# Transposing finished activation blocks with VectorE and device memory instead of TensorE, with four raw weight slots

## The reference, cut to what matters

```python
for l in range(2):
    h = rmsnorm(x, norm_mix[l])
    qa, ka, va, qi, ki, wi, qb, kb, vb = split(h @ w_in[l])
    o_a = dsa_branch(...)          # 8 heads x 128; keys chosen by an indexer score (qi, ki, wi), top 64 of 256
    o_b = swa_branch(...)          # 16 heads x 64, 2 kv heads, window of 128 keys, sinks
    g_a, g_b = split(sigmoid(h @ w_gate[l]))
    merged = g_a * (o_a @ w_branch_a[l]) + g_b * (o_b @ w_branch_b[l])
    x = x + merged @ w_out[l]
    h = rmsnorm(x, norm_mlp[l])
    x = x + square(relu(h @ w_up[l])) @ w_down[l]      # hidden width 8192
return rmsnorm(x, final_norm)
```

## Time and profile before

| | |
|---|---|
| median of 3 runs | 2830.13 us (2829.62 to 2831.28) |
| profiled execution: span, first to last instruction | 2829.1 us |
| TensorE busy / weight loads busy | 98% / 79% of the span |
| VectorE / ScalarE / GpSimd busy | 53% / 44% / 0% |
| mean granted TensorE clock | 0.994 |
| DMA | 506.41 MB, 54.1% of 16 engines' time |

### The profile page before, as it was taken

How to read it: one execution, slowest core, us unless ns; L and a number is a source line. 1 busy time by engine, 2 the same in 40 slices (tenths; PEclk the granted TensorE clock), 3 DMA queues, 4 the chain that set the end, 5 groups by cost and what they waited for, 6 DMA issues and landing times.

```text
span 2829.1 us, 37435 instructions
## 1 busy us (share of the span) xinstructions
PE 2784.3 (98%) x12610; PEld 2246.4 (79%) x12610; DVE 1503.9 (53%) x2106; ACT 1248.0 (44%) x1622; POOL 6.5 (0%) x16
## 2 busy tenths in 40 slices
PE   5999999999999999999999999999999999999998
PEld 4878778888888888888887887788888888888886
DVE  4575554555555555545555655545555455455554
ACT  3445454444444434434444455544444344343443
POOL 0000000000000000000000000000000000000000
PEclk8999999999999999999999999999999999999999
DMA  7644545555555555555554544455555555555553
GB/s 244 218 166 157 164 156 179 184 180 183 181 186 186 178 187 184 183 187 181 168 192 164 178 149 164 161 187 180 185 180 179 188 183 185 182 181 186 185 181 117
DMA packets 144951, 506.41 MB, mean 179 GB/s; under 512 B 15644, under 2 KB 21820, under 8 KB 144700
## 3 DMA queue, kind: packets, MB, share of 16 engines
q1 hardware_dynamic: 144828, 504.80, 54.1%
HBM read 497.92 MB, written 6.82 MB: 178 GB/s over the span
## 4 chain that ended last, share of the span: by engine, by line
issue 96%; DMA 2%; PE 1%; DVE 0%; ACT 0%; SPq 0%; POOL 0%; DVEq 0%; POOLq 0%; ACTq 0%
DMA raw<-in_w_main 1%; PE acc L340 0%; PE acc L341 0%; PE acc L342 0%; DMA bias_b<-bias_rows 0%; DMA raw<-in_w_misc 0%; DVE xs L1280 0%; ACT h_hl L766 0%; ACT w_hi L653 0%; DVE w_lo L918 0%; SPq L232 0%; SPq L258 0%; POOL bias_b L299 0%; POOL bias_b L298 0%; POOL root L291 0%
## 5 line engine op out<-in xcount | busy, mean ns | idle before, releaser
L918 DVE TENSOR_TENSOR w_lo<-raw,w_hi 128x1024 fp32r<-128x1024 f32 (+1 forms) x944 | 1146.5, 1218 | 1156.9 <-ACT w_hi L653 1153.5
L653 ACT ACTIVATE w_hi<-raw 128x1024 fp32r<-128x1024 f32 (+1 forms) x944 | 993.3, 1054 | 1317.5 <-PE acc L342 1279.0
L340 PE MATMUL acc<-w_hi,h_hl 128*128 128x512 f32 x2176 | 874.5, 402 | 20.2 <-DVE w_lo L918 20.2
L342 PE MATMUL acc<-w_hi,h_hl 128*128 128x512 f32 x2176 | 860.0, 395 | 0.0
L341 PE MATMUL acc<-w_lo,h_hl 128*128 128x512 f32 x2176 | 859.6, 395 | 0.0
L340 PE MATMUL acc<-w_hi,o_hl 128*128 128x512 f32 x1408 | 560.0, 398 | 0.0
L342 PE MATMUL acc<-w_hi,o_hl 128*128 128x512 f32 x1408 | 556.3, 395 | 0.0
L341 PE MATMUL acc<-w_lo,o_hl 128*128 128x512 f32 x1408 | 555.9, 395 | 0.0
L340 PEld LDWEIGHTS acc<-w_hi,h_hl 128*128 128x128 f32 x2176 | 409.7, 188 | 117.6 <-DVE w_lo L918 21.1
L342 PEld LDWEIGHTS acc<-w_hi,h_hl 128*128 128x128 f32 x2176 | 409.2, 188 | 97.8
L341 PEld LDWEIGHTS acc<-w_lo,h_hl 128*128 128x128 f32 x2176 | 409.9, 188 | 92.1
(11 more groups left out here) (141 smaller groups left out, 1029.7 us busy)
## 6 DMA issues: line engine op xcount, KB each, us to landing
raw<-in_w_main SPq DMA_DIRECT2D x928, 512.0 KB, 3.3
raw<-in_w_misc SPq DMA_DIRECT2D x16, 336.0 KB, 5.7
bias_rows<-stage SPq DMA_DIRECT2D x1, 4608.0 KB
xs<-in_x SPq DMA_DIRECT2D x4, 512.0 KB, 6.2
out<-xs SPq DMA_DIRECT2D x4, 512.0 KB, 2.9
bias_b<-bias_rows SPq DMA_DIRECT2D x1, 1536.0 KB, 11.5
bias_a<-bias_rows SPq DMA_DIRECT2D x1, 1024.0 KB, 7.2
qk<-in_final_gain SPq DMA_DIRECT2D x1, 1024.0 KB, 5.2
```

The source lines that it names most:

```text
L340: nc.tensor.matmul(o, a_hi, hi[:, kk], start=(k == 0), stop=False)
L342: last = nc.tensor.matmul(o, a_lo, hi[:, kk], start=False, stop=fin)
L653: nc.scalar.activation(w_hi[s][:, 0:2 * width], raw[r][:, 0:2 * width], ACT.Copy).then_inc(hi_ready, 1)
L918: nc.vector.tensor_tensor(w_lo[s][:, 0:2 * width], raw[r][:, 0:2 * width], w_hi[s][:, 0:2 * width].bitcast(F32), ALU.subtract).then_inc(lo ...
```

## The change

TensorE no longer transposes anything after the start (the fourth quarter of x in each layer's narrow chunks stays on it). Instead:

- In `take`, right behind the work that finishes the block, DVE transposes it in 32x32 blocks from [128 tokens, 512] into the tile `spread`, one instruction for each of the two token tiles (`spread_block`; `spread_keys` for the small keys). The output is written with elements 32 bytes apart.
- SP stores `spread` (512 KB, rows of 4 KB) to a device-memory tensor `scratch`, ahead of its load of chunk 7, and after its load of chunk 7 waits for the store and issues four fetches, each to 32 partitions in runs of 1 KB (`pass_on`). They land in the q/k tiles directly, or in `moved`.
- After their split of chunk 6 (hook `taken`), ACT makes the hi part from `moved` and DVE the lo part, for the whole block at once (`hi_moved`, `lo_moved`; for x, with its gains, in four pieces, `hi_moved_x`, `lo_moved_x`).
- The moved layout is [token, token tile, piece]: one channel block's 128 tokens lie 8 floats (32 bytes) apart. All stationary operands but the attention outputs are read with that stride, in the start's blocks too; so are queries and keys in the attention products, the small keys 16 bytes apart. `b_logits` makes its second key block with two matmuls instead of one.
- `RAW` is 4 instead of 8, to make room for `spread` and `moved`. SP's loads are written out by unit (`load_unit`), not in a loop of 8. The holds are at chunks 0 and 6.
- The 36 moves of a layer are 1 of keys, 8 of q/k columns, 27 of others (4 merged, 4 + 3 of x, 16 of the MLP).

```diff
-RAW = 8
+RAW = 4
+PIECES = NB // P
+QUARTERS = P // 32
...
-        h_hl = sb("h_hl", [P, 2, KT, SEQ], F32R)
+        h_hl = sb("h_hl", [P, 2, NBLK, P, TT, PIECES], F32R)
-        qk = sb("qk", [P, 2, A_HEADS, SEQ])
+        qk = sb("qk", [P, 2, 2, P, TT, PIECES])
+        kiT_kbT = sb("kiT_kbT", [P, P, TT, 2])
+        spread = sb("spread", [P, QUARTERS, 32, TT, PIECES])
+        moved = sb("moved", [P, P * TT * PIECES])
+        scratch = nc.dram_tensor("scratch", (P, NB * TT), F32, kind="Internal")
...
+            def load_unit(l, at, chunks, passing=None):
+                for c in range(chunks):
+                    if c == 7 and passing:
+                        passing[0]()
+                    sp.wait_ge(lo_ready, at + (l * CHUNKS + c + 1))
+                    sp.dma_start(raw[c % RAW][:], w_main[l, at + (c - N_MISC)]).then_inc(raw_in[c % RAW], 16)
+                if passing:
+                    passing[1]()
+            def pass_on(l, e, dst, pieces, g=0):
+                size = pieces * TT * 32
+                def store():
+                    sp.wait_ge(spread_ready, g * NBLK + (l * MOVES + e + 1))
+                    sp.dma_start(bass.AP(scratch, 0, [[NB * TT, P], [1, QUARTERS * size]]),
+                                 spread[:].rearrange("p j s t k -> p (j s t k)")[:, 0:QUARTERS * size]).then_inc(spread_stored, 16)
+                def fetch():
+                    sp.wait_ge(spread_stored, g * (NBLK * 16) + (l * (MOVES * 16) + (e + 1) * 16))
+                    for jj in range(QUARTERS):
+                        sp.dma_start(dst[32 * jj:32 * jj + 32],
+                                     bass.AP(scratch, jj * size, [[NB * TT, 32], [32 * NB * TT, QUARTERS], [1, size]]))\
+                            .then_inc(landed, 16)
+                return store, fetch
...
             def h_lhs(part, k, t):
-                return h_hl[:, part, k, t * P:(t + 1) * P]
+                return h_hl[:, part, k // PIECES, :, t, k % PIECES]
+            def moved_lhs(flat, k, t):
+                return flat.rearrange("p (s t k) -> p s t k", t=TT, k=PIECES)[:, :, t, k % PIECES]
+            def u_lhs(part, k, t):
+                return moved_lhs(o_moved[:, part, k // PIECES], k, t)
...
                 if j == 0:
-                    pe.wait_ge(turn_took, l * TURNS + (T_FIRST + T_QB + 4))
+                    pe.wait_ge(landed, l * (MOVES * LANDED) + (E_QB + 3) * LANDED)
...
-                    last = nc.tensor.matmul(att[g][:, 3 * P - WINDOW_KEYS:3 * P], q[:, P:SEQ], k[:, SEQ - WINDOW_KEYS:],
+                    nc.tensor.matmul(att[g][:, at:at + 64], q[:, :, 1], k[:, 64:P, 0], start=False, stop=False,
+                    last = nc.tensor.matmul(att[g][:, at + 64:3 * P], q[:, :, 1], k[:, :, 1], start=False, stop=True,
...
-                def turn_u(g, n, half):
-                    pe.wait_ge(squared, l * (GROUPS * NBLK) + g * NBLK + (n + 1))
-                    pe.wait_ge(turn_took, l * TURNS + g * 8 + (T_FIRST + T_U + 2 * n + half))
-                    for j in range(2):
-                        for t in range(TT):
-                            last = nc.tensor.transpose(turn[:, (j * TT + t) * P:(j * TT + t + 1) * P],
-                                                       stage_src(stage, half)(j, t), ident[:])
-                    last.then_inc(turned, 1)
...
-                    unit(..., o_lhs, ..., hold=[(0, turn_took, u0 + 6), (6, turn_took, u0 + 7), (7, turn_took, u0 + 8)] ...)
+                    unit(..., u_lhs, ..., hold=[(0, moved_took, g * NBLK + took_of(E_U + 2)), (6, moved_took, g * NBLK + took_of(E_U + 3))] ...)
...
                     split(cl, c, width, phase)
                     if turns and c in (5, 7):
                         turns((c - 5) // 2)
+                    if taken and c == 6:
+                        taken()
...
+            def hi_moved(l, e, dst, scale=1.0, g=0):
+                moved_ready(l, e, g)
+                nc.scalar.activation(dst, moved[:], ACT.Copy, scale=scale).then_inc(moved_hi, 1)
...
+            def spread_block(l, e, src, g=0):
+                spread_free(l, e, g)
+                if e >= E_M:
+                    dve.wait_ge(moved_took, g * NBLK + (l * TAKES + (e - E_M + NBLK)))
+                for t in range(TT):
+                    last = nc.vector.transpose(spread[:, :, :, t, :].rearrange("p j s k -> p k j s"),
+                                               src[:, t, :].rearrange("p (k j s) -> p k j s", k=PIECES, j=QUARTERS))
+                last.then_inc(spread_ready, 1)
+            def lo_moved(l, e, hi, lo, scale=1.0, g=0):
+                dve.wait_ge(moved_hi, g * NBLK + (l * TAKES + (e - E_M + 1)))
+                nc.vector.scalar_tensor_tensor(out=lo, in0=moved[:], scalar=scale,
+                                               in1=hi.bitcast(F32), op0=ALU.mult, op1=ALU.subtract).then_inc(moved_took, 1)
```

More of the change, by code:

```diff
@@ L238, in load_misc @@
                     sp.wait_ge(lo_ready, l * CHUNKS + (c + 1))
[L239 to L246, removed]
+                    sp.dma_start(raw[c % RAW][:, 0:2 * MISC], w_misc[l, c]).then_inc(raw_in[c % RAW], 16)
@@ L653, in split, with unit @@
                 nc.scalar.activation(w_hi[s][:, 0:2 * width], raw[r][:, 0:2 * width], ACT.Copy).then_inc(hi_ready, 1)
-            def unit(cl, chunks, take=None, turns=None, jobs=None, width=NB, phase=0, first=0):
+            def unit(cl, chunks, take=None, turns=None, taken=None, jobs=None, width=NB, phase=0, first=0):
                 for c in range(first, chunks):
@@ L763, in _ @@
                     act.wait_ge(turned, 2 * n + half + 1)
-                    for j in range(2):
-                        k = 4 * n + 2 * half + j
-                        last = nc.scalar.activation(h_hl[:, 0, k, :], first_turn[2 * n + half][:, j * SEQ:(j + 1) * SEQ],
-                                                    ACT.Copy, scale=gain[:, 0, k:k + 1])
-                    last.then_inc(turn_hi, 1)
+                    first_hi(first_turn[2 * n + half], n, half, lambda k: gain[:, 0, k:k + 1])
                 if n < 2:
@@ L848, in x_squares @@
                         square_block(n - 1, l * (2 * NBLK) + (NBLK + n - 1))
-                    unit(l * CHUNKS + (C_OUT + 8 * n), 8, take=x_squares if n else None, turns=x_out_turned)
+                    unit(l * CHUNKS + (C_OUT + 8 * n), 8, take=x_squares if n else None, taken=out_moved)
                 def take_up(g, n):
@@ L944, in hx @@
-            def hx(n, half):
-                return lambda part: h_hl[:, part, 4 * n + 2 * half:4 * n + 2 * half + 2, :]
+                    k = 2 * half + j
+                    hi, lo = (h_hl[:, part, n, :, :, k].rearrange("p s t -> p t s") for part in range(2))
+                    src = b[:, j * SEQ:(j + 1) * SEQ].rearrange("p (t s) -> p t s", t=TT)
+                    last = nc.vector.scalar_tensor_tensor(out=lo, in0=src, scalar=gain_of(PIECES * n + k),
+                                                          in1=hi.bitcast(F32), op0=ALU.mult, op1=ALU.subtract)
```

429 lines of the change are left out of this document (223 added, 206 removed).

## The result

The changed kernel takes 2984.02 us (median of 4 runs, 2982.77 to 2985.78), the kernel before 2830.11 us beside it (4 runs): a ratio of 1.054, 95% interval [1.053, 1.056]. It is slower by 154 us; I had forecast 2786 us and had put the upper end of the range at 2960. The profiled execution's span is 2984.1 us, 155.0 above the one of before.

The account below looks back on a forecast made before the run. TensorE's instruction stream was taken to pace everything; 2829.1 - 61.5 (transposes) + 0 (loads) + 5 (attention) + 3.5 (split) + 7 (start) + 2 (jitter) = 2785.1 us span, forecast 2786 us, range 2766 to 2960.

Parts of the forecast that it names:

- Removed from TensorE: TensorE's stream: 142 groups of four transposes go, each 0.433 us, saving 61.5 us in full.
- The weight loads with 32-byte stride: 10560 strided loads on TensorE stay hidden under matmuls of 0.233 us, up to 2.1 times the present pace: cost 0.
- my upper bound: Strided weight load: 1.82 ns an element, path 0.233 us, record 0.31 us, so 0.08 us exposed each, 845 us more.
- The rival that I gave 0.20: Strided load path exceeds 0.233 us under all 10560 matmuls; priced at 0.04 us each, +422, 3208 us; chance 0.20.
- Attention: Attention products: strided keys and queries as moving operands cost +5 us, at most +40 if reading doubles.
- The split: Mixer B's second key block, split in two, adds 32 matmuls with a load path of 0.11 us each: +3.5 us.
- VectorE: covered: 144 block transposes at 0.9 us (bound 1.4) add some 90 us busy time on an engine 53% busy, no delay.
- The round trip: Store and fetch through device memory land at T+12.3 after TensorE ends a unit at T; no stalls, 2.2 us spare.
- jitter: Allowance of +2 us for the round trip, whose margin was 2.2 us at the holds and 1 us for x blocks.
- comes too late: Rival: fetched blocks land at T+18 instead of T+12.3, stalling TensorE 122 us in all, 2906 us; chance 0.11.
- Four slots: Four raw slots: covered in the steady state; at the start the bias store goes out at about 25, costing +7 us.
- the sign that I gave: Sign of a right forecast at the start: one TensorE wait of about 27 us near the start.

Follow-up runs that it names:

- e7: The kernel before with the bias store issued by ScalarE on its own queue: 2810.6 us, ratio 0.993.
- e9: The changed kernel with blocks moved in runs of 32 tokens, all key, value, hidden and query operands dense, bias store on ScalarE's queue: 2765.1 us, ratio 0.977.
- e1: The changed kernel with the main products' stationary operands read from 128 neighbouring floats, writes and moves unchanged: 2841.4 us, ratio 1.003.
- e10: The changed kernel with the main products' stationary operands read 8 bytes apart, writes and moves unchanged: 2832.2 us, ratio 1.001.
- e3: The changed kernel with the main products' stationary operands read 16 bytes apart, writes and moves unchanged: 2919.1 us, ratio 1.032.
- e8: The changed kernel with queries and keys of the attention products read in neighbouring elements, main products left strided: 2935.6 us, ratio 1.037.
- e6: The changed kernel with blocks moved in runs of 32 tokens, main operands dense, queries strided, bias store on ScalarE's queue: 2793.5 us, ratio 0.987.
- e4: The kernel before with four raw slots instead of eight, bias tiles still behind 24 main chunks: 2838.2 us, ratio 1.003.
- e5: The changed kernel with blocks moved in runs of 32 tokens and main stationary operands written densely, queries still strided: 2814.3 us, ratio 0.994.

## Why the prediction was wrong

**What bounds the kernel, and what is paid ten thousand times: right.** "Anything that lengthens a matmul's distance" was the sentence that decided.

**Removed from TensorE, -61.5: right.** 20 matmuls on `turn` are left, as said. I had measured one group of four; all 142 in the trace of before, each less two matmul distances, sum to 61.8 us. Between e7 and e9, 45.5 us apart, the start distances of the matmuls on `turn` fall by 50.4 us and those of the main products beside them by 10.0; the second mixer's key products (+6.9), the waits for `w_lo` (+6.6) and the narrow chunks (+1.5) take some of it back.

**The weight loads with 32-byte stride, taken as 0: this step failed.** The claim was "up to 2.1 times the present pace it costs nothing", and that was sound; the load's path became 0.245 / 0.11 = 2.2 times as long. What was wrong is the argument for the pace. I took the moving operand's 0.46 ns a column as the pace "at which reading is possible" and concluded that a load has room to stride. But the moving operand of that row has neighbouring elements; it shows nothing of what a lone element costs. The measured cost is (331 - 188) / 128 = 1.1 ns a column more, over a dense path of 0.86. The pace of my upper bound, 1.82 ns a column, was nearly the truth: 0.245 / 128 = 1.9. There I erred the other way, by adding the 0.08 us between record and path to what sticks out: 13 ns do, not 80. The rival that I gave 0.20 is what happened, at 14 ns a load (142.6 us / 10368, by e1) instead of 40. By itself it would have stayed in the range, 2786 + 143 = 2929; the next two steps carried the time out of it. With the deciding ratio at 2.1 and no row on the stride, zero should not have been the forecast.

The Trainium skill, "SBUF — State Buffer", section "Door 1: The DMA port swizzle", was weighed and set aside. Its rule, at least two hits in a 16-byte line for full speed, is what e10 and e3 show: 196 ns with two floats in 16 bytes, 310 with one. Its sentence that one can stride freely over 4 fp32, read as a step of 4, does not hold for a load: that is the step of 16 bytes. "If it halves the pace, 0.22 us still fit" was my figure; it was 2.2 times.

**Narrow matmuls counted as if they had the same cover.** 192 of them were lumped into the 10560. A matmul of 336 columns covers 0.155 us, so each pays some 90 ns: 192 x 0.09 = 17 us that I overlooked (16.4 in the sums of starts). Half of it lies in the start, where it costs nothing extra, as said below.

**Attention, +5 with an upper bound of +40: wrong, and so was the bound.** Busy time rose by 39.3 + 12.7 = 52 us, cost by 48.5 (e8) and by the split block's 6.9. The 6.6 us of lower clock in it had no term at all: I allowed for the clock at the start only. I took keys and queries both for moving operands and asked what those cost. The queries are stationary: 320 + 64 matmuls of 64 to 256 columns, whose loads have almost no cover. In the sums of starts, 80.6 us after, 66.9 with dense keys (e6), 39.3 with dense queries as well (e9): keys 13.7, query loads 27.6. The split, booked at 3.5 for 32 loads, took 6.9: it adds 64 matmuls, and 64 x 0.11 = 7.0.

**VectorE: covered, as said.** Two transposes take 2.21 us, 1.1 each where I had 0.9 and a bound of 1.4; its busy time rose by 130 us instead of 90, on an engine that is 55% busy. My estimate from the Trainium skill ("VectorE: DVE Perf Modes", "The three transpose paths"), 4 x 0.311 = 1.24 us, is the nearer figure, but by luck. It ignores how the output is written. The same group, of the changed kernel and of e9, which writes runs of 32 floats:

```profile
L982 DVE STREAM_TRANSPOSE spread<-stage 128x512 f32<-128x512 f32 x112 | 123.8, 1192 | 37.5 <-ACT stage L826 26.1 <-DVE stage L1285 9.2 <-DVE stage L1238 1.7
```

```profile
L1004 DVE STREAM_TRANSPOSE spread<-stage 128x512 f32<-128x512 f32 x112 | 73.1, 690 | 32.0 <-ACT stage L838 20.3 <-DVE stage L1313 9.2 <-DVE stage L1266 1.8
```

Some 0.5 us of each transpose is the price of writing every float 32 bytes from the next.

**The round trip: right in its order, 1.6 us late, and covered.** Hi starts at T+13.9 (12.3 forecast), lo ends at T+16.2 against TensorE's T+17.8 (six chunks of 2.96 us). The changed kernel's slower pace gives a little of this cover. At the pace that I forecast it comes slightly late for two blocks of x, where I counted 1 us to spare: e1, with the same moves and nearly the old distance, waits for their lo parts twice, 2.9 us in all, close to the +2 that I had put for jitter. e9 shows no such wait, but its transposes are shorter. The rival "comes too late", priced at 122 us, is excluded.

**Four slots, +7: right for the slots alone, and not what the change shows.** e4 has +7.2. But the sign that I gave, a wait of about 27 us, did not come: it is 20.6. The bias store goes out 8.8 us later (26.82 instead of 18.04), and the narrow chunks of layer 0, with their longer loads, end 8.2 us later (last start 43.18 instead of 34.97). The two delays run side by side, and the first main matmul starts at 64.14 instead of 55.43: 8.7 us for both together.

**The sum.** In the sums of start distances, after against before: main products +140.5 us, matmuls on `turn` -49.9, narrow chunks +16.4, attention +48.1, waits -0.1. That is 155.0 us, the difference of the spans. Of the transposes' 61.8 us, 11.9 lie in the main products, so what was added to these is 140.5 + 11.9 = 152.4 us: 136 for 10368 loads (246.4 instead of 233.3 ns, the mean distances between 800 and 1300 us, without the matmuls next to a transpose), 6.6 of lower clock, and some 10 that I can't assign.

## What to carry over

Before an operand's layout is changed, ask for each operand on TensorE whether it is stationary or moving and how long the matmul is that must hide its load; short matmuls (narrow tiles, attention products, transposes) pay first and in full. A pace read from a dense operand is no evidence for a strided one: when the cover is a factor of two and the row is missing, the forecast belongs on the paying side. If a layout must be strided somewhere, put the stride on the copy that ScalarE or VectorE makes anyway, and keep what TensorE reads at two floats or more in 16 bytes.

## What the runs showed of the hardware

- A 128-column fp32r load is recorded with 189, 196, 310 and 331 ns at 4, 8, 16 and 32 bytes between its floats (e1, e10, e3, the change). The matmul's distance is then 0.232, 0.232, 0.240 and 0.246 us: two floats in 16 bytes cost nothing here, one does, and a longer step costs a little more again.
- Where loads set the pace, a load's record is 85 ns longer than the time until the next can start at 32 bytes (331 against 246, the change) and 70 ns longer at 16 (310 against 240, e3). The idle time ahead of the PEld groups (92.1 us before, 3.1 after, for the middle one of the three `h_hl` groups) tells sooner than any length whether loads set the pace.
- The granted clock fell to 0.50 for 3.4 us in four places behind attention matmuls with strided queries and keys, which cost 6.6 us in all (the change). e1, e3 and e10, with the same attention, have two, two and one such stretch outside the start and the end; e8, with dense attention reads, e5 and e6, with strided queries alone, and the kernel before have none. What in these matmuls brings the clock down was not tested. TensorE's busy share shows nothing of it: it is 100% in the stretches.
- A 32x32-block transpose of 128x512 fp32 on VectorE takes 1.19 us with its output floats 32 bytes apart (the change) and 0.69 us in runs of 32 floats (e9).
- One 4.6 MB store at the head of a queue held the loads behind it for 20 us (e7), though both orders move the same bytes over the same 16 engines.
- Open: with loads well covered, the matmul distance is not always the same. Between 800 and 1300 us it alternates between 229 and 238 ns in e5, e6 and e9 (mean 233.3), and is 232.4 in e1 and 231.6 in e10, at a granted clock of 1.00 in all. Over 11,000 matmuls that is 10 to 19 us, and none of the runs was made to tell its cause; e1's 142.6 us may hold some of it.
